# A third out-gate unit between levels 5 and 6, and level 6 taken out of PSUM before the chunk queries are scaled

## What is computed

```python
def chunked_gated_linear_recurrence(q, k, v, g, s0, scale):
    def step(S, inp):
        qc, kc, vc, gc = inp
        b = jnp.cumsum(gc, axis=1)
        decay = jnp.exp(jnp.where(mask, b[:, :, None] - b[:, None, :], -jnp.inf))
        attn = jnp.einsum('bthk,bshk,btshk->bhts', qc, kc, decay) * scale
        o_intra = jnp.einsum('bhts,bshv->bthv', attn, vc)
        o_inter = jnp.einsum('bthk,bhkv->bthv', qc * jnp.exp(b), S) * scale
        b_last = b[:, -1]
        k_dec = kc * jnp.exp(b_last[:, None] - b)
        S_new = S * jnp.exp(b_last)[..., None] + jnp.einsum('bshk,bshv->bhkv', k_dec, vc)
        return S_new, o_intra + o_inter
...
    o = rms_norm(o, gn) * jax.nn.silu(heads(g, GLA_DV))     # g: the out gate
    return o.reshape(B, T, GLA_VAL_DIM) @ w_out, s
```

## Time and profile before

| | |
|---|---|
| median of three runs | 2336.67 us (2335.9 to 2337.2) |
| the profiled execution | 2337.72 us, its span 2336.0 us |
| mean granted TensorE clock | 0.986 of full speed |
| TensorE matmul busy | 2256.5 us, 97% of the span |
| VectorE busy | 1581.4 us, 68% |
| ScalarE busy | 1078.2 us, 46% |
| GpSimd busy | 422.7 us, 18% |
| DMA moved | 213.33 MB, mean 91 GB/s |

### The profile page before, as it was taken

How to read it: one execution, slowest core, us unless ns; L and a number is a source line. 1 busy time by engine, 2 the same in 40 slices (tenths; PEclk the granted TensorE clock), 3 DMA queues, 4 the chain that set the end, 5 groups by cost and what they waited for, 6 DMA issues and landing times.

```text
span 2336.0 us, 41750 instructions
## 1 busy us (share of the span) xinstructions
PE 2256.5 (97%) x17519; PEld 2200.8 (94%) x17519; DVE 1581.4 (68%) x2148; ACT 1078.2 (46%) x1543; POOL 422.7 (18%) x283
## 2 busy tenths in 40 slices
PE   7999999989899999999999999998988999999998
PEld 6999999879899999999999999987987899999998
DVE  7888833546468888535788873368577678886344
ACT  5555623333345555423555552254354455555234
POOL 5222201101021221201122220012011112222001
PEclk9999999999999999999999999999999999999999
DMA  3333333224243333333233342322232233333331
GB/s 112 109 102 98 103 90 89 82 64 122 64 113 84 99 106 101 91 93 91 64 100 109 92 116 76 90 76 60 81 97 82 56 97 106 100 100 100 100 87 52
DMA packets 385753, 213.33 MB, mean 91 GB/s; under 512 B 6960, under 2 KB 379343, under 8 KB 385567
## 3 DMA queue, kind: packets, MB, share of 16 engines
q1 hardware_dynamic: 385344, 210.59, 31.9%
q0 software_dynamic: 32, 0.03, 0.0%
q10 hardware_dynamic: 190, 0.05, 0.0%
HBM read 198.98 MB, written 11.67 MB: 90 GB/s over the span
## 4 chain that ended last, share of the span: by engine, by line
PE 85%; DVE 7%; ACT 4%; issue 2%; POOL 1%; DMA 0%; SPq 0%; ACTq 0%; DVEq 0%; POOLq 0%
PE ps L544 39%; PE ps L597 35%; PE ps L730 5%; POOL hidden L2119 1%; DVE hid_low L1646 1%; DVE w_low L1520 1%; PE ps L767 1%; DVE ex L1833 1%; PE ps L823 1%; ACT w_high L1063 1%; PE ps L888 1%; DVE gate_sum L1841 1%; PE ps L808 0%; PE ps L903 0%; DMA x_tok<-in_x_sample_dram 0%
## 5 line engine op out<-in xcount | busy, mean ns | idle before, releaser
L597 PE MATMUL ps<-u_diffs,w_high 128*128 128x272 f32 x2560 | 487.2, 287 | 2.8 <-ACT ps L1162 2.8
L597 PEld LDWEIGHTS ps<-u_diffs,w_high 128*128 128x128 f32 x2560 | 401.6, 188 | 3.5 <-issue 3.5
L597 PE MATMUL ps<-u_diffs,w_low 128*128 128x272 f32 x1280 | 368.8, 288 | 0.0
L2119 POOL TENSOR_TENSOR hidden<-t_gate,t_up 128x544 f32<-128x544 f32 x88 | 229.2, 2605 | 764.9 <-ACT t_gate L1185 764.9
L1520 DVE TENSOR_TENSOR w_low<-w_raw,w_high 128x1024 fp32r<-128x1024 f32 x205 | 265.7, 1311 | 108.9 <-ACT w_high L1063 108.7
L544 PE MATMUL ps<-hid_high,w_high 128*128 128x272 f32 x1408 | 291.2, 288 | 3.8 <-DVE w_low L1520 2.1
L544 PE MATMUL ps<-hid_high,w_low 128*128 128x272 f32 x1408 | 289.5, 288 | 0.0
L544 PE MATMUL ps<-hid_low,w_high 128*128 128x272 f32 x1408 | 289.2, 287 | 0.0
L597 PE MATMUL ps<-u_high,w_low 128*128 128x272 f32 x960 | 278.3, 290 | 0.0
L597 PE MATMUL ps<-u_high,w_high 128*128 128x272 f32 x960 | 275.2, 287 | 0.7 <-DVE w_low L1616 0.7
L597 PE MATMUL ps<-u_low,w_high 128*128 128x272 f32 x960 | 275.8, 287 | 0.0
(11 more groups left out here) (261 smaller groups left out, 4195.8 us busy)
## 6 DMA issues: line engine op xcount, KB each, us to landing
w_raw<-in_ffn_w_gu_dram SPq DMA_DIRECT2D x176, 512.0 KB, 5.1
w_raw<-in_ffn_w_down_dram SPq DMA_DIRECT2D x64, 512.0 KB, 4.6
w_raw<-in_hgrn_w_in_dram SPq DMA_DIRECT2D x32, 512.0 KB, 4.1
w_raw<-in_gla_w_in_dram SPq DMA_DIRECT2D x25, 512.0 KB, 4.1
w_raw<-in_ffn_w_down_dram SPq DMA_DIRECT2D x32, 384.0 KB, 4.3
w_raw<-in_ple_w_gate_dram SPq DMA_DIRECT2D x16, 512.0 KB, 4.5
states_s<-in_state_gla_dram SPq DMA_DIRECT2D x8, 512.0 KB, 4.5
out_gla_s_dram<-states_s SPq DMA_DIRECT2D x8, 512.0 KB, 3.5
```

The source lines that it names most:

```text
L597: mm = pe.matmul(ps[:, bank, 0:HALF], half_slot(w, base, h)[:, k * P:(k + 1) * P], x(k), start=start and k == 0 and part == 0, stop=k == K ...
L2119: pool.tensor_tensor(HID[:, f, :], tG[:, :], tU[:, :], ALU.mult).then_inc(s["hid_mul"], 1)
```

## The change

Three edits. Out-gate tile g2 moves out of `mix` into `Group.steps`, between levels 5 and 6, on all engines: TensorE multiplies it there, ScalarE and VectorE prepare the unit two ahead of it there, and VectorE takes g1 out of PSUM before level 6's work instead of behind it. In `mix`, g3 takes the place that g2 had, in front of the key transposes, and nothing stands any more between attention times values and the state updates. On VectorE, level 6 is taken out of PSUM before the chunk queries are scaled, not behind them.

```diff
-        self.steps = [("g", 0, ("diag",)), ("v", 0, (0,)), ("v", 1, (1,)), ("v", 2, (2,)), ("v", 3, (3, 4)), ("g", 1, (5, 6))]
-        self.g2_unit = self.start + self.nfeat + 6
+        self.steps = [("g", 0, ("diag",)), ("v", 0, (0,)), ("v", 1, (1,)), ("v", 2, (2,)), ("v", 3, (3, 4)), ("g", 1, (5,)), ("g", 2, (6,))]
+        self.g3_unit = self.start + self.nfeat + 7
...
 # TensorE, mix
-            feature_tile(gr, gr.nfeat + 2, gr.g2_unit)
+            feature_tile(gr, gr.nfeat + 3, gr.g3_unit)
 
             pe.wait_ge(s["kdec_made"], gi + 1)
             pe.wait_ge(s["lvl_out"], LEVELS * gi + 6)
...
                 keys(1)
-
-            feature_tile(gr, gr.nfeat + 3, gr.g2_unit + 1)
 
             pe.wait_ge(s["kd_out"], N_KD[gi + 1])
             update(0)
...
 # ScalarE, mix
-            ahead(gr.g2_unit)
+            ahead(gr.g3_unit)
...
-            ahead(gr.g2_unit + 1)
             for part in range(NH // 2):
...
 # VectorE, mix
-            ahead(gr.g2_unit)
+            ahead(gr.g3_unit)
...
+            level_out(gr, LEVELS - 1)
             dve.wait_ge(s["chunk_exp"], gi + 1)
             dve.tensor_tensor(Q[:, 0:NH * T], Q[:, 0:NH * T], EP[:, 0:NH * T], ALU.mult)\
                .then_inc(s["qin_made"], 1)
-            level_out(gr, LEVELS - 1)
             dve.wait_ge(s["qin_made"], gi + 1)
 
-            ahead(gr.g2_unit + 1)
-            for j in (2, 3):
-                feature_out(gr, gr.nfeat + j, gr.g2_unit + j - 2, OG[:, 4 * gr.g + j, :])
+            feature_out(gr, gr.nfeat + 3, gr.g3_unit, OG[:, 4 * gr.g + 3, :])
```

## The result

The changed kernel takes 2317.05 us (median of four runs, 2316.7 to 2318.6), the kernel before 2336.93 beside it. The ratio is 0.9917, with a 95% interval of 0.9905 to 0.993: 19.9 us faster. The profiled execution took 2317.29 us, its span is 2315.6 us. Two executions of later runs, 3628.9 us of the changed kernel and 10739.0 us of e10, stand far outside all others and are left out of every median here.

What follows compares the result with a forecast made beforehand. TensorE at work sets 85% of the end, so only its waits and slow stretches can pay. Gains of 22.8 us at full clock, less 4.5 for low clock and 0.6 for VectorE, make 17.7: 2319.0 us, range 2316 to 2322.

Steps and rivals of the forecast that it cites:

- The GLA groups: Groups 0 and 1, level 5 to first state update: TensorE runs without a stop, 5.5 us gained each.
- The HGRN groups: Groups 2 and 3: VectorE's chain sets the times; new length 24.6 us, gains 5.1 and 6.7 us.
- The three waits of the plan: HGRN groups, TensorE: 1.1 us for the transposes, 0.9 for level 6 out, 1.4 for ScalarE's copy.
- VectorE beside GpSimd: Low part inserted before level 6 is held up by GpSimd's product: 0.3 us per HGRN group, bounds 0 and 1.1.
- The clock that stays: Low TensorE clock remains under g2 in some groups and perhaps under attention times values: 4.5 us lost in all.
- the 25 to 27: Expected us between level 5 and the first update in the HGRN groups of the changed profile.
- Rival 1: The clock stays high once g2 fills the hole between levels: 4.5 us more gained, 2314.5 us; chance 0.27.
- what follows moves forward as a whole: Behind the state updates nothing depends on absolute times, so no gain or loss was counted there.
- The moved loads: Sample-state loads, issued 2 and 3.4 us later in group 0, still land before they are needed: no cost.
- rival 2: The wait only moves back on VectorE, to the transposes: 11.4 us gained, 2325.3 us; chance 0.19.
- rival 4: Level 6 out still ends late, waiting for products behind g2; all gains halved for unseen reasons: 2331 us; chance 0.04.

Runs made afterwards that it cites:

- e10: The change with one VectorE low part later and, in the HGRN groups, discarded matmuls in the waits before level 5 and the first unit of values: 2310.45 us.
- e5: The change, with the low part before the suffix differences moved behind level 6 out and the chunk queries on VectorE: 2315.76 us.
- e1: The change without its VectorE reordering: g2 moved, but level 6 still taken out behind the chunk queries: 2329.76 us.
- e7: The change, with the low part between levels 5 and 6 on VectorE made behind level 6 instead: median 2324.64 us.
- e2: The kernel before, with only level 6 taken out before the chunk queries; g2 and g3 stay where they were: 2333.87 us.
- e3: The change, but g3 stays between attention times values and the state updates: 2343.45 us, ratio to before 1.0029.
- e6: e5 with the sample-state products put in front of the first updates in the HGRN groups: 2315.93 us.
- e4: The kernel before, with extra matmuls, results thrown away, in TensorE's wait before level 6: 2335.36 us.

## Why the prediction was right

The time, 2317.05 against 2319.0 us, is inside the range. The mechanism was right, and one term of the sum was wrong. That the forecast came as near as 2.0 us is partly luck: without the wrong term the sum gives 2314.5, off by 2.6 the other way, and most of that difference lies outside the four stretches.

- **The GLA groups.** 5.5 us each by the plan; measured 5.2 and 5.1. The whole queue from level 5 on runs without a stop, with slack at each place that the prediction counted: the keys are ready at 490.6 and g2 ends at 492.3, the decayed keys are made at 498.2 and g3 ends at 499.4. The missing 0.3 to 0.4 us are TensorE's own time, 18.6 instead of 18.25.
- **The HGRN groups.** 5.1 and 6.7 us by the plan, 5.0 and 6.7 measured. The new length was to be 24.6 us and is 24.5. The three waits of the plan, 1.1, 0.9 and 1.4 us (L802, L823, L808), are 0.96, 0.62 and 1.11. e5 shows that VectorE's chain sets the first, and e1 that the second edit is what keeps the one at L823 short.
- **VectorE beside GpSimd.** I took 0.3 us per HGRN group of the bounds 0 and 1.1. The low part was held up by 1.13 us, the differences behind it were free for it, and the sum is nearly 0. e7 shows why.
- **The clock that stays.** This is the term that failed: "I count one for the two GLA groups, ... and one for each HGRN group", 4.5 us. It measured nothing: in neither profile of the changed kernel did the clock fall in any of the four stretches, and the HGRN groups came to 24.5 us, below the 25 to 27 that the prediction named as its sign. The step behind it was that group 2's clock, low right behind a 2.06 us wait, would be low again. Level 5's own products run before any second hole can count. In the HGRN groups they were slow in 7 of 20 cases with that hole open: once in the kernel before, twice each in e2 and e3, once each in e5 and e6, never in e1, e4, e7 or the two profiles of the change. In the GLA groups, where the hole is 1.66 us, level 5's products were slow in none of 24. The case is one of chance, and I priced it as a rule. As an estimate, 7 in 20 at the 1.57 us that it cost e5 make 1.1 us for both HGRN groups, against the 2.2 that I counted there. Rival 1 was right about the stretches.
- **A reading that was off.** The prediction sets timeline rows of 3.78 and 2.56 us beside a row of the chain, 1.78. Read from the timeline too, 16 such products take 1.95 to 2.05 us at full clock. So they were slow by 1.7 to 1.8 and 0.5 us, not 2.0 and 0.8. The sum does not use these figures.
- **What made up for it.** Outside the four stretches the profiled execution lost 1.5 us: the stretches between groups 0 and 1, 1 and 2, and the end of the program are 0.7, 1.2 and 2.0 us longer, the one between groups 2 and 3 is 2.6 shorter. The last is one unit of values at full clock, 7.22 us where it took 9.86 before. Low-clock stretches lie elsewhere in each profile. The prediction said that what follows moves forward as a whole; it does, but single units change by up to 2.6 us with the clock.
- **The other rivals.** The moved loads cost nothing in the change, and e6 shows how near they are: TensorE is ready for them 3.0 us earlier than in e5, and one group waits. The wait moving back on VectorE (rival 2) is what e3 and e1 show: it comes if either the place or the order is left out. Of rival 4 there is no sign: TensorE waits 0.62 us for level 6's eviction. Its 2331 does not follow exactly either; 22.8 halved, less the other terms, leaves 6.3 us, so 2330.4.

## What to carry to other kernels

When a unit of work is moved to cover a wait, ask what stood behind it: the work behind must move up too, or the hole only changes place, as e3 shows with +6.6 us instead of -19.9. A hole of two to three us on TensorE can cost about as much again in clock, as in the GLA groups with 2.3 and 2.6 us, but it does not do so each time. Two edits that each close one of two holes in a chain bring more together than the sum of their parts (in the four stretches 21.9 against 17.8 us). Where a hole can't be filled with useful work, matmuls whose results are thrown away can keep the clock up behind it, but time is gained only if no later hole grows by what they save.

## What the runs showed of the hardware that I had not expected

- TensorE's clock does not fall behind every hole of the same length. The 2.06 us wait before level 5 of the HGRN groups was followed by the low clock in 7 of 20 cases, the 1.66 us one of the GLA groups in none of 24. One of 2.26 us in e7, 16 us behind the last hole, was followed by it in both groups, and so was one of 2.9 us in e1 and e4. Whether two holes near each other count for more than one was not tested.
- In front of the first unit of values in the HGRN groups, a wait of 3.5 us was followed by the low clock in 11 of 11 cases, one of 2.5 to 2.7 us in 5 of 13.
- Executions of one kernel can differ by 5 to 6 us along with the mean clock (e7: 2319.0 at 0.994, 2324.0 to 2325.4 at 0.991).
- A VectorE instruction that collides with GpSimd's product takes 1.1 us longer (1.22 to 2.35 us for a low part, 1.28 to 2.40 for two differences); put another one first and the second runs at full speed.
